# Three hand-overs to TensorE re-ordered in a two-block transformer kernel: attention's values in pieces, differential attention's operands ahead of the gates' logarithm, the last mLSTM head's fills and norm moved

## The reference

```python
def first_block(x, ...):
    h = rms_norm(x, norm_mix_pre[l])
    c_q, c_kv, k_rope, sc_b, sc_c, sc_h, ssd_in = jnp.split(h @ w_in[l], IN_SPLITS, axis=-1)
    y_att = mla_mixer(c_q, c_kv, k_rope, cos, sin, ...)     # 8 heads, causal softmax, 96 wide keys, 64 wide values
    y_conv = short_conv_mixer(sc_b, sc_c, sc_h, sc_conv_w[l])
    y_ssd = ssd_mixer(ssd_in, ...)
    x = x + rms_norm(jnp.concatenate([y_att, y_conv, y_ssd], axis=-1) @ w_out[l], norm_mix_post[l])
    h = rms_norm(x, norm_ffn_pre[l])
    u = causal_dwconv(h @ ffn_w_up[l], ffn_conv_w[l]) + ffn_conv_b[l]
    gate, up = jnp.split(u, 2, axis=-1)
    return x + rms_norm((jax.nn.silu(gate) * up) @ ffn_w_down[l], norm_ffn_post[l])

def second_block(x, ...):
    proj = _rmsnorm(x, norm_pre[l]) @ w_in[l]
    qa, ka, va, za, qb, kb, vb, ob, zb, igb, fgb, ga, gb = _split(proj, sizes)
    oa = _rmsnorm(_diff_attention(qa, ka, va, lam), norm_a[l]) * (1.0 - lam_init)   # 4 heads, ALiBi bias
    ya = oa * jax.nn.silu(za)
    hb = _mlstm(silu(conv(qb)), silu(conv(kb)), vb, ig, log_sigmoid(fg))            # 4 heads of 128
    yb = _rmsnorm(jax.nn.sigmoid(ob) * hb, norm_b[l]) * jax.nn.silu(zb)
    merged = jax.nn.sigmoid(ga) * (ya @ w_a[l]) + jax.nn.sigmoid(gb) * (yb @ w_b[l])
    return x + _rmsnorm(merged @ w_out[l], norm_post[l])
```

## Time and profile before

| | us |
|---|---|
| median of three executions | 2355.34 (2355.04 to 2357.51) |
| the profiled execution | 2356.65 |
| its span | 2354.8 |
| TensorE busy | 2241.4 (95%) |
| TensorE's weight loads busy | 1737.9 (74%) |
| VectorE / GpSimd / ScalarE busy | 1171.3 / 1019.8 / 716.1 |
| mean granted clock of TensorE | 0.985 of full |

### The profile page before, as it was taken

How to read it: one execution, slowest core, us unless ns; L and a number is a source line. 1 busy time by engine, 2 the same in 40 slices (tenths; PEclk the granted TensorE clock), 3 DMA queues, 4 the chain that set the end, 5 groups by cost and what they waited for, 6 DMA issues and landing times.

```text
span 2354.8 us, 27395 instructions
## 1 busy us (share of the span) xinstructions
PE 2241.4 (95%) x9862; PEld 1737.9 (74%) x9862; DVE 1171.3 (50%) x1239; ACT 716.1 (30%) x1131; POOL 1019.8 (43%) x821
## 2 busy tenths in 40 slices
PE   6999999889899999999999987999999998999998
PEld 5777755567688888888887766777767776788877
DVE  5864355536663333333334787666665455411123
ACT  4343255533311111111112343555344333200112
POOL 2533410167554444444444662222244552444475
PEclk8999999999999999999999998999999999999999
DMA  5111100032211111111111230000101111111143
GB/s 196 54 36 36 36 10 10 10 134 81 63 54 53 45 53 45 45 53 45 53 45 45 76 142 28 28 27 27 36 28 45 45 40 32 45 45 47 51 161 116
DMA packets 34031, 130.61 MB, mean 55 GB/s; under 512 B 4132, under 2 KB 4516, under 8 KB 33196
## 3 DMA queue, kind: packets, MB, share of 16 engines
q1 hardware_dynamic: 30960, 111.39, 14.7%
q10 hardware_dynamic: 3004, 18.30, 2.1%
HBM read 117.04 MB, written 12.58 MB: 55 GB/s over the span
## 4 chain that ended last, share of the span: by engine, by line
PE 82%; DVE 9%; ACT 4%; issue 3%; DMA 1%; POOL 1%; SPq 0%; DVEq 0%; ACTq 0%; POOLq 0%
PE PG L666 13%; PE PG L672 13%; PE PG L671 13%; PE PG L1192 5%; PE PG L1198 5%; PE PG L1197 5%; PE PG L1013 2%; PE PO L1040 1%; PE PO L1263 1%; PE PT L1027 1%; PE PG L719 1%; PE PG L724 1%; PE PG L725 1%; DMA WR<-weights 1%; PE PO L764 1%
## 5 line engine op out<-in xcount | busy, mean ns | idle before, releaser
L559 POOL TENSOR_TENSOR WH<-WR,zero 128x512 fp32r<-128x512 f32 x380 | 418.1, 1100 | 1230.0 <-PE PG L666 679.6
L562 POOL TENSOR_TENSOR WL<-WR,WH 128x512 fp32r<-128x512 f32 x380 | 540.0, 1421 | 29.8
L666 PE MATMUL PG<-HH,WH 128*128 128x512 f32 x1136 | 449.2, 395 | 3.2 <-issue 2.3
L672 PE MATMUL PG<-HH,WL 128*128 128x512 f32 x1136 | 443.0, 390 | 0.0
L671 PE MATMUL PG<-HL,WH 128*128 128x512 f32 x1136 | 442.6, 390 | 0.0
L666 PEld LDWEIGHTS PG<-HH,WH 128*128 128x128 f32 x1136 | 213.7, 188 | 52.4 <-issue 6.2
L671 PEld LDWEIGHTS PG<-HL,WH 128*128 128x128 f32 x1136 | 213.8, 188 | 46.1 <-issue 2.2
L672 PEld LDWEIGHTS PG<-HH,WL 128*128 128x128 f32 x1136 | 213.6, 188 | 44.8
L1192 PE MATMUL PG<-HH,WH 128*128 128x512 f32 x544 | 229.1, 421 | 5.4 <-ACTq L2025 2.7
L1198 PE MATMUL PG<-HH,WL 128*128 128x512 f32 x544 | 214.6, 394 | 0.0
L1197 PE MATMUL PG<-HL,WH 128*128 128x512 f32 x544 | 214.1, 394 | 0.0
(11 more groups left out here) (535 smaller groups left out, 4147.8 us busy)
## 6 DMA issues: line engine op xcount, KB each, us to landing
WR<-weights SPq DMA_DIRECT2D x196, 512.0 KB, 3.5
RAW<-x SPq DMA_DIRECT2D x8, 512.0 KB, 8.0
x_spill<-X ACTq DMA_DIRECT2D x1, 4096.0 KB, 12.8
X<-x_spill ACTq DMA_DIRECT2D x1, 4096.0 KB, 12.1
x_spill<-X ACTq DMA_DIRECT2D x4, 1024.0 KB, 5.4
X<-x_spill ACTq DMA_DIRECT2D x8, 512.0 KB, 3.9
y<-RAW SPq DMA_DIRECT2D x7, 512.0 KB, 5.1
POSI<-positions ACTq DMA_DIRECT2D x1, 512.0 KB, 15.4
```

Source lines behind the costliest of these rows:

```text
L559: pool.tensor_tensor(WH[:, slot, part], WR[:, slot, part], zero[:, :].to_broadcast([P, HALF]), ALU.add).then_inc(w_hi, 1)
L562: pool.tensor_tensor(WL[:, slot, part], WR[:, slot, part], WH[:, slot, part].bitcast(F32), ALU.subtract).then_inc(w_split, 1)
L666: m = pe.matmul(out[:, cut], WH[:, slot, w], hi[:, cut], start=n == 0, stop=False)
L672: m = pe.matmul(out[:, cut], WL[:, slot, w], hi[:, cut], start=False, stop=last)
```

## The change

It does five things.

1. Attention: `values(0)` is cut into four pieces, one for each block of keys. The first stands before tile 4's transposes, the others between the two heads' transposes of tiles 4, 5 and 6. The blocks of the first four tiles lie in the other half of PTB. The next pair's scores and exponentials of tile 0 come before this pair's late values.
2. Differential attention: ScalarE copies the AUG rows (before, VectorE did), makes the operands first and takes the gates' exponential and logarithm after them; SiLU comes ahead of the gates' DMA. On VectorE the low parts precede the softplus.
3. Last mLSTM head: fills 0 and 1 at tile 0, one at tile 2, one at tile 3, and none at tiles 4 to 7; merge gates 0 and 1 together on ScalarE.
4. The column sums of the last head's norm run between the fourth and the fifth block of the first merge projection, into PT.
5. The mixers wait for four parts of y at a time.

```diff
@@ -676,11 +676,17 @@
-            def projection(stage, g, k, u, hi, lo, i=0, stride=0, between=lambda: None):
+            def projection(stage, g, k, u, hi, lo, i=0, stride=0, between=lambda: None, early=lambda: None):
+                def second():
+                    unit(stage, u, i, stride, 1)
+                    early()
...
                 product(g.psum(k), [(slot, b, hi[:, b, :], lo[:, b, :]) for b in range(KT)],
-                        w_used[1], (1, KT // 2), lambda: unit(stage, u, i, stride, 1), between).then_inc(g_ready, 1)
+                        w_used[1], (1, KT // 2), second, between).then_inc(g_ready, 1)
@@ -1005,7 +1011,7 @@
-                def scores(t, hh):
+                def scores(t, hh, i=i):
                     n = mla_group(i, t, hh)
@@ -1028,26 +1034,33 @@
-                def values(h):
-                    pe.wait_ge(t_free, i * 24 + (8 if h == 0 else 24))
-                    if h == 0:
+                def value(h, j):
+                    a = max(0, j * P - h * HALF)
+                    for hh in range(2):
+                        at = (2 * i + hh) * 64
+                        m = pe.matmul(PO[hh * 64:(hh + 1) * 64, h, a:HALF], VP[:, j, at:at + 64],
+                                      PTB[:, hh, j + 4 * (1 - h), a:HALF], start=j == 0, stop=j == 4 * h + 3)
+                    return m
+                def early_values(j):
+                    if j == 0:
+                        pe.wait_ge(t_free, i * 24 + 8)
                         primed(pe, att_free, i)
                         pe.wait_ge(n_done, NDONE["ssd"])
-                    for j in range(4 * h + 4):
-                        a = max(0, j * P - h * HALF)
-                        for hh in range(2):
-                            at = (2 * i + hh) * 64
-                            m = pe.matmul(PO[hh * 64:(hh + 1) * 64, h, a:HALF], VP[:, j, at:at + 64],
-                                          PTB[:, hh, j, a:HALF], start=j == 0, stop=j == 4 * h + 3)
-                            if j == 4 * h + 3:
-                                m.then_inc(pv_half, 1)
-                pe.wait_ge(krot_done, 2 * i + 2)
+                    value(0, j).then_inc(pv_half, 1)
+                def late_values():
+                    pe.wait_ge(t_free, i * 24 + 24)
+                    for j in range(TT):
+                        m = value(1, j)
+                    m.then_inc(pv_half, 1)
                 if i == 0:
+                    pe.wait_ge(krot_done, 2)
                     Groups("kv").wait_free(pe, 6)
                     Groups("kv").wait_free(pe, 7)
-                for hh in range(2):
-                    scores(0, hh)
+                    for hh in range(2):
+                        scores(0, hh)
                 for t in range(TT):
@@ -1056,10 +1069,16 @@
                     if t == 4:
-                        values(0)
+                        early_values(0)
+                    transposes(t, 0)
+                    if 4 <= t < 7:
+                        early_values(t - 3)
+                    transposes(t, 1)
+                if i < 3:
+                    pe.wait_ge(krot_done, 2 * i + 4)
                     for hh in range(2):
-                        transposes(t, hh)
-                values(1)
+                        scores(0, hh, i + 1)
+                late_values()
@@ -1289,7 +1308,6 @@
-            pe.wait_ge(aug_k, 1)
             with pe.Fori(0, DIFF_HEADS - 1) as i:
@@ -1370,7 +1388,7 @@
                     if last:
-                        next_head(max(j - 4, 0), max(j - 3, 0))
+                        next_head(*{0: (0, 2), 2: (2, 3), 3: (3, 4)}.get(j, (0, 0)))
                     else:
@@ -1404,27 +1422,37 @@
                     next_head(20, 24)
+                if last:
+                    return
                 pe.wait_ge(m_sq, i + 1)
-                spread(hb, 4 if last else 12, ones, SQ[:, 0, :])
+                spread(hb, 12, ones, SQ[:, 0, :])
...
+            hb = Halves("mlstm", ML_HEADS - 1, ML_HALVES)
+            for m in (2, 3):
+                hb.wait_free(pe, m)
+            g = Groups("merge_first")
+            def last_norm():
+                pe.wait_ge(m_sq, ML_HEADS)
+                for m in (4, 5):
+                    hb.before(pe, m)
+                    pe.matmul(PT[:, m % 2, :], ones, SQ[:, 0, halves(m)], start=True, stop=True)                      .then_inc(hb_ready, 1)
+            projection("merge", g, 0, 2, HH, HL, early=last_norm)
             primed(pe, m_pp, ML_HEADS * TT)
+            projection("merge", g, 1, 3, HH, HL)
             for m in (4, 5):
-                Halves("mlstm", ML_HEADS - 1, ML_HALVES).wait_free(pe, m)
-            g = Groups("merge_first")
-            for k in range(2):
-                projection("merge", g, k, 2 + k, HH, HL)
-            wait_split("y")
+                hb.wait_free(pe, m)
             def mixers(g, k, u, i=0, stride=0):
...
                     slot = unit("merge", u, i, stride, n)
+                    pe.wait_ge(s_lo, SPLIT0["y"] + 4 * n + 4)
                     g.before(pe, k + n)
@@ -1766,7 +1794,7 @@
-                def exp(t, hh):
+                def exp(t, hh, i=i):
                     n = mla_group(i, t, hh)
@@ -1779,15 +1807,18 @@
                         act.wait_ge(t_ready, i * 24 + (n + 1))
-                        if t % 4 == 0 and q == 0:
-                            primed(act, pv_half, i * 4 + (1 + hh if t else 0))
-                        m = min(4, t + 1 - 4 * q)
-                        act.activation(PTB[:, hh, 4 * q:4 * q + m, (t % 4) * P:(t % 4 + 1) * P],
+                        if t == 0:
+                            primed(act, pv_half, 5 * i)
+                        if q == 1:
+                            primed(act, pv_half, 5 * i + t - 3)
+                        m, at = min(4, t + 1 - 4 * q), 0 if t >= 4 and q == 0 else 4
+                        act.activation(PTB[:, hh, at:at + m, (t % 4) * P:(t % 4 + 1) * P],
                                        PT[:, n % 2, 0:m * P].rearrange("p (b n) -> p b n", b=m),
...
-                exp(0, 0)
-                exp(0, 1)
+                if i == 0:
+                    exp(0, 0)
+                    exp(0, 1)
                 for t in range(TT):
@@ -1795,7 +1826,10 @@
                         act.dma_start(X[:, :, :].rearrange("p k n -> p (k n)"), spill).then_inc(x_back, 16)
-                primed(act, pv_half, 4 * i + 4)
+                if i < 3:
+                    exp(0, 0, i + 1)
+                    exp(0, 1, i + 1)
+                primed(act, pv_half, 5 * i + 5)
                 act.activation(RAW[:, i, :], POf, ACT.Copy).then_inc(att_free, 1)
@@ -1921,12 +1955,7 @@
             act.activation(cols[:, 8:10], cols[:, 8:10], ACT.Exp).then_inc(lam_exp, 1)
-            log1p_rows(1, flat, 2)
-            wide = Wide(DIFF_WIDE)
-            wide.ready(act, 0)
-            act.activation(NK[:, :], wide.psum(0), ACT.Copy).then_inc(wide.free(0), 1)
             g.wait_free(act, 1)
-            wide.wait_free(act, 0)
@@ -1941,18 +1970,27 @@
             queries_high(QHL, d_qhi)
+            act.wait_ge(aug_k, 1)
+            act.wait_ge(lam_loaded, 80)
+            for rows, c in ((slice(64, 66), 0), (slice(0, 2), 1)):
+                act.activation(QHA[rows, c, :], AUG[rows, 0, :], ACT.Copy)
+                act.activation(KLA[rows, c, :], AUG[rows, 1, :], ACT.Copy, scale=0.25)
+            wide = Wide(DIFF_WIDE)
+            wide.ready(act, 0)
+            act.activation(NK[:, :], wide.psum(0), ACT.Copy).then_inc(wide.free(0), 1)
+            wide.wait_free(act, 0)
             keys_high()
...
             act.sem_inc(wide.free(1), 1)
-            act.wait_ge(aug_k, 1)
             queries_high(QHA, d_qb)
+            log1p_rows(1, flat, 2)
+            g.ready(act, 2)
+            act.activation(RAW[:, 0, :], g.psum(2), ACT.Silu).then_inc(g.free(2), 1)
             act.wait_ge(forget_made, 1)
...
                 act.dma_start(GROWS[2][at:at + 4, :], flat[0]).then_inc(forget_back, 16)
-            g.ready(act, 2)
-            act.activation(RAW[:, 0, :], g.psum(2), ACT.Silu).then_inc(g.free(2), 1)
@@ -2132,12 +2170,11 @@
                         merge_gate(0)
+                        merge_gate(1)
                     if not last and j in (2, 4, 5, 6, 7):
...
                             next_half(m)
-                if last:
-                    merge_gate(1)
-                else:
+                if not last:
                     act.wait_ge(m_scores, i * TT + TT)
@@ -2147,6 +2184,7 @@
                     merge_gate(2)
+                    merge_gate(3)
                 else:
@@ -2161,9 +2199,7 @@
                 act.activation(SQ[:, 0, :], MH[:, :], ACT.Square).then_inc(m_sq, 1)
-                if last:
-                    merge_gate(3)
-                else:
+                if not last:
                     for m in (10, 11):
@@ -2173,7 +2209,7 @@
                     hb.ready(act, m)
```

(16 more changed lines are left out.)

## The result

| | before | after |
|---|---|---|
| median of the executions, us | 2356.43 (2355.04 to 2357.83) | 2322.56 (2320.08 to 2323.91) |
| profiled execution, its span | 2356.65, 2354.8 | 2321.32, 2319.5 |
| TensorE busy | 2241.4 | 2231.7 |

The account below looks back on a forecast made before the run. TensorE, busy 95% of the span, bounds the kernel, so only its waits and low clock can give. 12.2 + 6.5 + 12.4 = 31.1 us off the 2355.34 us median gives 2324.3 us; range 2319 to 2330, up to 2336 with rivals.

Parts of the forecast that it names:

- Attention: Four pairs of heads: value pieces in the transposes' waits plus new order between pairs, 12.2 us less (bounds 5 and 14).
- The pieces: Attention, tiles 4 to 6: cut early values hide TensorE's waits, 1.36 us a pair, 5.4 us over four.
- The boundaries: Between attention pairs: next scores ahead of late values, 4.8 us over three, plus 2.0 at the third; 6.8 us.
- Rival 4: Attention: each of 24 added switches into PO restarts the array; at 2 us each slower, 2372 us; chance 0.03.
- First operands: Before differential attention's first scores: ScalarE makes operands first, TensorE starts earlier; 6.5 us less (bounds 2 and 8.5).
- Two idles of 1.4 us: Differential attention: TensorE would idle 1.4 us before the first scores and 1.4 us awaiting the first exponentials.
- rival 2: ScalarE's table changes cost more than their load; two before SiLU cost 2.6 us, giving 2326.9 us; chance 0.05.
- Last head and merge: Last mLSTM head to mixers: fills into waits, norm's sums moved, mixers' wait halved; 12.4 us less (bounds 6 and 15).
- The fills: Last mLSTM head: fills moved into the 4.64 and 2.68 us waits, so the remaining fills end 9.3 us earlier.
- the two new waits: Last mLSTM head: first fill's bank free 0.9 us after the scores; exponential of maxima 0.55 us after TensorE's next scores.
- The norm: Merge: norm's sums inside the projection, mixers waiting for the fourth low part; 3.1 us less, some 1.9 us idle left.
- rival 1: Remaining short idles (1.4, 1.4, 1.9 us) let the clock fall; gain only 24, 2331.5 us; chance 0.13.

Follow-up runs that it names:

- e6: The differential-attention part alone (e3) with SiLU put back behind the gates' DMAs; 2353.89 us, ratio 0.9985.
- e4: Kernel before with only the last mLSTM head's, norm's and merge's part of the change; 2342.98 us, ratio 0.9947.
- e7: e4 with the fills and merge gate 1 back in their old places, norm move and mixers' half waits kept; 2354.10 us, ratio 0.9981.
- e9: Changed kernel with the first merge gate's sigmoid ahead of y's splits on ScalarE; 2321.60 us, ratio 0.9865.
- e1: Kernel before with only the attention's part of the change; 2344.54 us, ratio 0.9955.
- e2: e1 with the four value pieces in one block ahead of tile 4's transposes, leaving only the boundaries' new order; 2348.48 us, ratio 0.9973.
- e5: Kernel before with only group 2's SiLU moved ahead of the gates' DMAs on ScalarE; 2353.89 us, ratio 0.9990.
- e3: Kernel before with only the differential attention's part of the change; 2346.01 us, ratio 0.9960.
- e8: Changed kernel with the mixers waiting for all eight parts of y; 2325.12 us, ratio 0.9859.
- e10: The changed kernel itself measured again, beside e9; 2323.60 us, ratio 0.9869.

## Why the prediction was right, and where not

**Attention, 12.2 forecast, 11.6 measured.** The pieces gave 4.9 us (forecast 5.4), the waits at tiles 5 and 6 stand at 0.26 and 0.39 (0.4 and 0.5). The boundaries gave 6.7 (6.8), but the near hit is in part luck. The forecast had 2.0 us at the last one, 1.7 of clock and 0.3 of waits, put down to GpSimd's split. The fall there cost 1.0 us (43.14 us from the third pair's late values to the fourth's before, 42.13 in e6), and four kernels with the same boundary and the same split, e4 to e7, did not have it; the rest of that boundary's extra was 0.8 us. Without the fall the boundaries give 5.6 us. Rival 4 (a price for each switch into PO) falls: the pieces and the transposes around them overlap without a gap in the first fence above.

**First operands, 6.5 forecast, 8.6 measured: the term that was mis-sized.** The direction and the chain were right. Two idles of 1.4 us were forecast; 0.71 us and none came. What failed is the sum along VectorE. Counted from the moment that ScalarE is free (1394.80 before, 1383.52 after), I had the keys' low parts end at 13.8 us, and they ended at 12.6 (ScalarE's copies follow each other a little closer, and the subtractions took 3.61 us, not 4.17); I had the softplus finished 8.6 us later, and it took 7.8. So TensorE met no wait for the first maximum, and the exponentials came 3.1 us behind the first scores, under a fill, in place of 4.8. The softplus took less because one step took 0.18 us (1402.19 in VectorE's timeline above) where it had taken 0.96:

```profile
1406.59 0.96 DVE L2372 TENSOR_SCALAR FLAT<-FLAT 128x32 f32<-128x32 f32 x1
```

The softplus steps of 0.9 us and more all lie beside GpSimd's splits, and so do a few short ones; GpSimd stands idle from 1402.10 to 1404.72 in the changed kernel, and all eight steps that begin from 1402.19 to 1403.75 take 0.18 or 0.19 us. That another engine's work sets the length of these steps fits the traces and is not shown: no run moved the splits alone.

**The table loads** cost their 1.28 us and no more: the logarithm starts 0.01 us behind its load. The Trainium skill (ScalarE: Activation LUTs, section What ACT_TABLE_LOAD costs) adds a drain of about 1380 ns to each switch; this trace does not show it, and rival 2 falls.

**Last head and merge, 12.4 forecast, 12.5 measured.** The fills gave 9.9 us for 9.3: the two new waits are 0.30 and 0.53 us, not 0.9 and 0.55, and 4.64 + 2.68 + 3.4 - 0.83 is 9.9. The norm gave 2.6 for 3.1: the wait ahead of the mixers, ended by ScalarE behind the first sigmoid as forecast, is 2.49 us and not 1.9, since the chain from the sums to the mixers took 23.4 us where the one to that sigmoid's end had taken 22.7. That tiles 4 to 7 need no fill as cover held: TensorE has no idle above 0.1 us there.

**What the sum left out: 3.1 us between the first operands and the last head.** The instructions there are the same. Before, the clock fell behind two idles of 2.33 and 1.97 us, ahead of the scores at 1446.05 and 1467.43; after, it does not, behind idles of the same length. By the scores' starts, one such stretch takes 1467.43 - 1446.05 = 21.38 us with a fall and 1446.11 - 1426.32 = 19.79 without, 1.6 us each. My argument on rival 1, "2.29 did not, 2.68 did", looked like a limit in length and is none, as the last section shows. Rival 1 did not come true, but that no short idle cost anything in the first profile (1.00 behind 2.49 us) was in part luck. So by the traces 31.1 - 0.6 + 2.1 + 3.1 + 0.1 = 35.8 us, the four columns' difference; the medians show 33.9, since the stretches not shown take back 0.4, the profiled execution of the changed kernel lies 1.2 us under its median, and that of the kernel before 0.2 over.

## What to carry to other kernels

A step that is put ahead on one engine gives its gain only if everything between it and the waiting engine goes ahead too: here two reorderings worth 1.2 and 3.9 us alone made 8.6 together, since each left the other's last link in place. Cover a wait with pieces of work that are already due (a value's block, a fill), no larger than the wait; and before removing a wait, look at what ends just behind it, as e9 shows. A change of less than 2 us cannot be read here from medians, since single falls of the clock cost 1.0 to 2.5 us; stage lengths of the traces show it, once each is checked for a fall.

## What the hardware did that was not expected

Equal idles come with and without a fall of TensorE's clock. Three idles of about 2 us stand in all traces in front of the same instructions; the stretches of 3 us behind them in the kernel before, the changed kernel and its repetition:

```profile
1446.05:1449.05 3.00, 3.00 (x11) 0.67 0.49 180
1467.43:1470.43 3.00, 3.00 (x8) 0.52 0.62 175
2240.43:2243.43 3.00, 3.00 (x13) 1.00 0.00 0
```

```profile
1426.32:1429.32 3.00, 3.00 (x15) 1.00 0.62 183
1446.11:1449.11 3.00, 3.00 (x14) 1.00 0.59 175
2205.07:2208.07 3.00, 3.00 (x13) 1.00 0.00 0
```

```profile
1425.85:1428.85 3.00, 3.00 (x15) 1.00 0.56 183
2204.64:2207.64 3.00, 3.00 (x10) 0.74 0.00 0
```

| idle, us | fell | did not fall |
|---|---|---|
| 2.3 (differential attention) | before, e1, e2, e4, e5, e6, e7 | after, e3, e8, e9, e10 |
| 2.0 (20 to 21 us later) | before, e2, e5, e6, e7 | after, e1, e3, e4, e8, e9, e10 |
| 1.8 (a later product with y) | e1, e7, e8, e9, e10 | before, after, e2, e3, e4, e5, e6 |
| 0.7 twice (the old attention's last boundary) | before, e3 | e4, e5, e6, e7 |

At 1.8 us of idle the same program fell in one execution and not in another (after and e10). At 2.3 us the fall went with the order: in all seven kernels whose first scores had come after 3.96 us of idle or more, in none of the five with 0.68 to 0.71. Whether that earlier idle is the cause, or the moment at which the short one begins, stays open: no run moved one without the other. At the attention's last boundary, two idles of 0.74 and 0.67 us, the fall came in two of six executions with the same instructions on every engine up to there, so there the order does not decide.
